# Which weight chunks of a mixture of experts are multiplied as whole float32

## The reference

```python
def swiglu(x, w1, w2):
    gate, up = jnp.split(x @ w1, 2, axis=-1)
    return (jax.nn.silu(gate) * up) @ w2

def moe_ffn(x, router_w, w1, w2):
    ...
    top_logit, top_idx = lax.top_k(logits, TOP_K)       # TOP_K = 2 of 8 experts
    gates = jax.nn.softmax(top_logit, axis=-1)
    ...
    def expert_group(args):
        x_blk, e = args
        return swiglu(x_blk, w1[e], w2[e])              # w1[e] 1024 x 5632, w2[e] 2816 x 1024
```

## Time and profile before

| | us |
|---|---|
| median of 3 runs | 1419.19 |
| lowest and highest of the runs | 1417.68, 1422.4 |
| the profiled execution, its own time | 1417.29 |
| its span | 1415.1 |

### The profile page before, as it was taken

One profiled execution on the slowest core, in us unless ns is written; L12 is line 12 of the kernel. 1 busy time (PEld: TensorE's weight loads), 2 busy tenths in 40 slices (PEclk: granted clock), 3 DMA queues, 4 the chain that ended last, 5 costly groups with the idle time before them and its releaser, 6 DMA issues.

```text
span 1415.1 us, 18950 instructions
## 1 busy us (share of the span) xinstructions
PE 1384.8 (98%) x7443; PEld 1139.5 (81%) x7443; DVE 1107.9 (78%) x1187; ACT 909.9 (64%) x1008; POOL 52.3 (4%) x58
## 2 busy tenths in 40 slices
PE   7999999999999999999999999999999999999997
PEld 7999898888888998989776768777687767877775
DVE  7868665666645787865588889988899888998897
ACT  6746444555534756344467778877788777877775
POOL 0031000000000022000000000000000000000000
PEclk9999999999999999999999999999999999999998
DMA  8433453455555443353569999999999999999993
GB/s 312 160 127 118 151 177 113 156 179 188 198 181 188 172 146 104 135 178 126 231 240 401 400 400 405 423 402 380 405 404 423 399 376 411 403 423 399 378 414 150
DMA packets 54480, 388.36 MB, mean 274 GB/s; under 512 B 6000, under 2 KB 6256, under 8 KB 8176
## 3 DMA queue, kind: packets, MB, share of 16 engines
q1 hardware_dynamic: 53840, 384.98, 70.3%
q10 hardware_dynamic: 544, 2.10, 0.4%
HBM read 386.00 MB, written 1.05 MB: 274 GB/s over the span
## 4 chain that ended last, share of the span: by engine, by line
issue 51%; PE 47%; DVE 2%; DMA 0%; ACT 0%; POOL 0%; POOLq 0%; DVEq 0%
PE pb L1249 10%; PE pb L1250 10%; PE pb L1251 10%; PE pb L1545 5%; PE pb L1546 3%; PE pb L1397 1%; PE pb L1479 1%; PE pb L1499 1%; PE pb L1230 1%; PE pb L1548 1%; DVE xTb L1919 1%; DMA h<-in_x 0%; PE pb L1489 0%; PE pb L1455 0%; PE pb L1456 0%
## 5 line engine op out<-in xcount | busy, mean ns | idle before, releaser
L1870 DVE TENSOR_TENSOR wlo<-raw,whi 128x2048 fp32r<-128x2048 f32 (+1 forms) x101 | 225.9, 2246 | 107.6 <-ACT whi L750 107.3
L750 ACT ACTIVATE whi<-raw 128x2048 fp32r<-128x2048 f32 (+1 forms) x101 | 189.9, 1882 | 148.9 <-PE pb L1251 116.0
L820 ACT ACTIVATE whi<-raw 128x2048 fp32r<-128x2048 f32 x91 | 172.7, 1913 | 42.3 <-PE pb L1251 29.7
L1949 DVE TENSOR_TENSOR wlo<-raw,whi 128x2048 fp32r<-128x2048 f32 x73 | 165.3, 2282 | 16.8 <-ACT whi L820 16.6
L1249 PE MATMUL pb<-xTb,whi 128*128 128x256 f32 x384 | 110.0, 287 | 1.8 <-DVE xTb L1907 1.2
L1545 PE MATMUL pb<-xTb,whi 128*128 128x512 f32 x308 | 111.0, 399 | 0.2
L1250 PE MATMUL pb<-xTb,whi 128*128 128x256 f32 x384 | 108.6, 283 | 0.0
L1251 PE MATMUL pb<-xTb,wlo 128*128 128x256 f32 x384 | 108.6, 283 | 0.0
L1711 PE MATMUL pb<-whi,xg 128*128 128x512 f32 x264 | 107.1, 406 | 0.0
L1949 DVE TENSOR_TENSOR kvXr<-kvX,whi 128x2048 fp32r<-128x2048 f32 x42 | 95.4, 2282 | 12.1 <-ACT whi L820 12.1
L1546 PE MATMUL pb<-xTb,wlo 128*128 128x256 f32 x352 | 91.6, 281 | 0.0
(11 more groups left out here) (459 smaller groups left out, 3488.0 us busy)
## 6 DMA issues: line engine op xcount, KB each, us to landing
raw<-in_ffn_w SPq DMA_DIRECT2D x179, 1024.0 KB, 7.5
raw<-in_lin_w SPq DMA_DIRECT2D x64, 1024.0 KB, 4.9
kvX<-in_ffn_w SPq DMA_DIRECT2D x60, 1024.0 KB, 8.0
arena<-in_ffn_w SPq DMA_DIRECT2D x58, 1024.0 KB, 8.0
raw<-in_lin_w SPq DMA_DIRECT2D x4, 536.0 KB, 5.5
arena<-in_mem ACTq DMA_DIRECT2D x2, 1024.0 KB, 8.1
h<-in_x SPq DMA_DIRECT2D x1, 1024.0 KB, 5.2
out<-xn SPq DMA_DIRECT2D x2, 512.0 KB, 4.0
```

What stands on the lines that cost most here:

```text
L750: nc.scalar.activation(whi[:, m % HRING, c], raw[:, m % RING, c], ACT.Copy).then_inc(hi_ready, 1)
L820: nc.scalar.activation(high_home(p, n), xraw_slots[slot], ACT.Copy).then_inc(hi_ready, 1)
L1870: V.tensor_tensor(wlo[:, m % RING, c], raw[:, m % RING, c], whi[:, m % HRING, c].bitcast(F32), ALU.subtract).then_inc(lo_ready, 1)
L1949: V.tensor_tensor(xlo_slots[slot], xraw_slots[slot], high_home(p, n).bitcast(F32), ALU.subtract).then_inc(lo_ready, 1)
```

## The change

`WHOLE` names two steps in place of five, and `WHOLE2` is 2 in place of 3. Per pair the full expert has four whole chunks in place of eight: the second chunks of steps 4, 6 and 9 and the chunk 24 of the second layer are split. From `WHOLE2` also follows that the hidden activations of step 2 get a high and a low part (float32r) in place of one float32 copy, and that `xhTf` is shorter.

```diff
 LAG = 3
 LIGHT = P // 2
-WHOLE = (4, 5, 6, 8, 9)
-WHOLE2 = 3
+WHOLE = (5, 8)
+WHOLE2 = 2
```

## The result

| | before | after |
|---|---|---|
| median of 4 runs each, us | 1419.29 | 1406.91 |
| lowest and highest | 1417.68, 1422.4 | 1406.04, 1407.9 |
| the profiled execution, its own time | 1417.29 | 1407.64 |
| its span | 1415.1 | 1405.5 |

The ratio is 0.9913, with a 95% interval of 0.9894 to 0.9932: faster by under one per cent, 12.4 us between the medians and 9.6 us between the two profiled executions. 1407.9 was predicted, with 1404.8 to 1415.

What follows compares the result with a forecast made beforehand. The prediction took TensorE to bound the kernel. Twelve first-layer chunks at 0.71 us (8.5) and four second-layer ones at 0.70 (2.8) save 11.3 us: 1419.19 - 11.3 = 1407.9 us, range 1404.8 to 1415.

Steps and rivals of the forecast that it cites:

- What bounds the kernel: In a whole pair, TensorE sets the pace, busy for all of its 172.40 us; its producers wait for it.
- 0.71 and 0.70 us per chunk: TensorE's saving per chunk turned from whole to split: 0.71 us in the first layer, 0.70 in the second.
- The four passes: On TensorE, true float32 as four array passes: a whole chunk of 3.63 us, not 3.43, and 14.5 us for sixteen.
- The sum, 11.3 us: TensorE's total saving: twelve first-layer chunks give 8.5 us, four second-layer chunks 2.8, together 11.3.
- VectorE's walk through turn 3: VectorE followed back to back from chunk 8's low part: no stall, least slack 0.36 us, at chunk 10.
- The step that I had called the weakest: The walk through turn 3 takes for granted that ScalarE's high parts are always there when VectorE comes to them.
- The new wait of the transposes of step 3: TensorE's transposes wait for VectorE's added low part, written in turn 3 and reached at about 919; nothing queues behind it.
- The region behind turn 13: VectorE's walk around turns 9 to 13, chunk 24 split behind two whole ones: about 1 us left at the least.
- ScalarE and the loads: ScalarE has room in each turn; a pair's loads take 167 us at 415 GB/s, against a pair of 169.6.
- B: VectorE's cushion a little short: TensorE waits at chunk 10 and behind turn 13, 1 us per pair, 1412 us; chance 0.14.
- C: Loads are the bound at what they now reach, 402 GB/s: time stays at 1419, or 1413 to 1416; chance 0.12.
- D: VectorE becomes the bound in turns without a whole chunk: some 6 us of stall per pair, 1432 us; chance 0.07.

Runs made afterwards that it cites:

- e1: Changed kernel with three whole second-layer chunks kept, so only the first-layer part of the change: 1409.81 us, 0.9934 of the kernel before, pair 170.30 us.
- e2: Changed kernel with whole first-layer chunks at steps 4, 5, 6, 8, 9, so only the second-layer part: 1418.88 us, 0.9993 of before, pair 171.73 us.
- e5: Changed kernel with no whole first-layer chunk and VectorE copying in place of subtracting for low parts (wrong results): 1398.85 us, pair 168.20 us.
- e11: The changed kernel itself, run once more on another chip: 1409.73 us, 0.9923 of the kernel before, pair 169.87 us.
- e7: Changed kernel with whole first-layer chunks at steps 4 and 8 in place of 5 and 8: 1406.09 us, 0.9905 of before, pair 169.57 us.
- e3: Changed kernel with no whole chunk in the first layer, two in the second: 1417.09 us, 0.9975 of before, pair 172.10 us.
- e9: Changed kernel with one whole first-layer chunk, at step 6, in place of 5 and 8: 1406.95 us, 0.9912 of before, pair 170.13 us.
- e4: Changed kernel with one whole second-layer chunk in place of two (chunk 23 split as well): 1410.44 us, 0.9938 of before, pair 170.57 us.
- e6: Like e5, also without the third matmul of the full expert's first-layer chunks (wrong results): 1383.55 us in one run, pair 164.63 us.
- e8: Changed kernel with step 3's gating product made three more times, 1.35 us more VectorE work in turn 3: 1412.63 us, 0.9951 of before.

## Why the prediction was right, point by point

**What bounds the kernel.** Right: TensorE. e1 and e2 move by the number of its chunks, and e5 shows that lifting a producer brings TensorE's own time and no more.

**0.71 and 0.70 us per chunk.** Right to 0.02: 2.73 in place of 3.43, 3.08 in place of 3.77. The four passes of the Trainium skill (FP8 and Floating Point Precision, TensorE Precision Notes) would by the estimate in the prediction have given 14.5 us for sixteen chunks; the measured differences give 11.3, so these runs don't agree with a plain 4/3. Four passes themselves are not contradicted: a quarter of a whole matmul is 3.43 / 16 = 0.214 us, and one matmul of a split product is 2.72 / 12 = 0.227. What breaks the 4/3 is that the split's matmuls come 0.013 us further apart than these quarters; no run asks why.

**The sum, 11.3 us.** Right in the steady part, three pairs with 3 x 2.83 = 8.5 less three waits of 0.23, 7.8 as measured. The spans differ by 9.6 and not by 11.3 for these reasons: on one side the waits (0.7) and the start, where three chunks less (2.1 us) came out as only 0.3 because chunk 4 and the gathering around it ran 1.8 us longer, at a granted clock of 0.78 from 726 to 732 us where it had been 1.00; and on the other side a last store to memory that took 3.1 us in place of 4.0. The medians differ by 12.4, more than the sum. The executions of one kernel scatter by some us with the mean granted clock (the numbers of e11 are at the end), so it is partly luck that the median came within 1.0 us of the forecast. (The lower end of the range, 1404.8, is 1404.7 by its own terms, which changes nothing.)

**VectorE's walk through turn 3.** The sequence came as written (the starts 914.06 to 921.93 above are those of the walk, moved by 0.73), the margin did not: 0.36 us was predicted, and TensorE's chunk 10 ended 0.23 later than it could have, in three pairs, where I had put the weak place. The step was mis-sized by two terms. The slack at chunk 8, from which I walked, was 3.26 from VectorE's start to TensorE's (910.39 to 913.65), and it is 3.02 now (909.66 to 912.68): it is itself a product of the whole chunks of the pair before. The other traces bear that out: 3.26 in e1, with three whole chunks in the second layer, 3.03 in e2 and e7, with two, 2.84 in e3 and e9, with two there and fewer in the first layer, and 2.49 in e4, with one. And I took a low part as ready at the next start on VectorE; the trace shows TensorE starting at 922.15, 0.22 behind 921.93. 0.36 - 0.24 - 0.22 is -0.10, and the first three matmuls after such a wait take 0.77 (922.15 to 922.92) in place of 0.68: together 0.19 of the 0.23. The step that I had called the weakest held: ScalarE's high parts were there each time, for VectorE stands back to back from 909.66 to 921.93. The new wait of the transposes of step 3 cost nothing, as said: L2505 starts at 914.39, the transposes at 918.13.

**The region behind turn 13.** About 1 us was to be left at the least, and no wait was found there. It held for the change, though the margin was thinner than said: the expectation of e4 puts it at 0.6 in the trace after. e4 and e9 show that it was the next to go, by 0.4 to 0.8 a pair at the light transposes ahead of chunk 25.

**ScalarE and the loads.** Right, and the loads were held too dear: 167 us for a pair in the prediction's sum, 164.6 measured in e6. The 358 GB/s of the Trainium skill (SBUF — State Buffer, Summary: rules for kernel authors) would have made 193 us; e6 doesn't agree, with 422 GB/s over 158 us.

**The rivals.** B, that TensorE waits a little at chunk 10, happened at a quarter of its price. C is refuted by e6. D: its mechanism is real and begins right behind the change (e3: VectorE 169 of 172 us busy, 3.9 us of waits per pair); by distances of starts its price was near, by full durations, by which D was priced, it was not. e8 shows what decides: once the cushion is gone, VectorE's microseconds are TensorE's, one for one, until the next whole chunk.

**What would show it.** 64 records each of the whole matmuls were announced; from the instructions of their lines in the trace after, the three groups of L1714 adding up to 64:

```profile
L1714 PE MATMUL pb<-arena,xgf x24: 590/592/592, 758.9 to 1267.4; 128*128 128x512 f32 x24
...
L1714 PE MATMUL pb<-kvX,xgf x24: 590/592/592, 789.1 to 1301.2; 128*128 128x512 f32 x24
...
L1714 PE MATMUL pb<-raw,xgf x16: 590/592/593, 958.8 to 1097.7; 128*128 128x512 f32 x16
```

```profile
L1741 PE MATMUL pb<-raw,arena x64: 592/592/697, 817.8 to 1337.8; 128*128 128x512 f32 x64
```

## What to carry to other kernels

A slower form on the bounding engine that spares the others is a purchase of slack: here 0.7 us of TensorE bought 2.2 us of VectorE and 1.8 of ScalarE. It pays only where a producer would else be late, so walk the producer's fixed order turn by turn against the consumer's and buy just ahead of the place where the walk runs out (step 4 rather than 5, 0.3 us a pair). Take the starting slack with care, since it depends on what was bought before, and add some 0.2 us for the handoff from VectorE to a waiting TensorE (0.22 in the changed kernel and in e8). And compare such versions by a distance inside the trace, between two instructions that come once per round: whole runs here scatter by more than what sets e7, e9 and the changed kernel apart.

## What the runs showed of the hardware

- TensorE's granted clock falls for some us at the start of the experts, where TensorE has a row of short waits, and where and for how long differs between executions of the same work: 0.72 and 0.74 between 720 and 726 us in before and after and 1.00 in e11; 1.00, 0.78 and 0.84 between 726 and 732 us; 0.50, the lower of its two levels, in the next 6 us of e11. The work of e11 up to the first selection took 5.9 us longer than in the first profile of the same kernel (812.5 against 806.6), and all behind it the same time. Six executions of e11 lie at 1411.8 to 1413.8 where the mean clock of the execution was 0.991 or 0.992, and at 1406.1 to 1407.7 where it was 0.995 or 0.996.
- One core drew 422 GB/s from memory for 158 us on end in loads of 1 MiB, while TensorE was busy for 148.5 us of them and ScalarE for 138.9 (e6). The DMA share was 1.01 there, and 1.00 at 402 GB/s in before.
- On VectorE a copy of 128 x 2048 float32 into float32r takes 1.23 us (e5), a subtraction of two such operands 2.28 (before).
- A whole float32 matmul of 128 x 512 takes 3.43 / 4 = 0.86 us against 2.72 / 4 = 0.68 for the three matmuls of a split product (before).
